# Modulation products of a fused two-block kernel taken from unsplit fp32 weights in four column groups, with six weight chunks in flight and two waits moved

## The reference

```python
for l in range(2):
    mod_lat = silu(c)     @ w_mod[l] + b_mod[l]    # [1024] @ [1024, 6144]
    mod_ctx = silu(c_ctx) @ w_mod[l] + b_mod[l]
    # shift, scale, gate for the mixer; shift, scale, gate for the MLP
    h = rms_norm(x, g) * (1 + scale) + shift
    x = x + gate * rms_norm(mixer(h), g_post)      # l=0: grid attention, l=1: gated linear attention
    x = x + gate * rms_norm(square(relu(h2 @ w_mlp_in)) @ w_mlp_out, g_post)
```

## Time and profile before

| | |
|---|---|
| executions | 2675.56, 2680.70, 2681.21 us (median 2680.7) |
| the profiled execution | 2680.21 us, of which the span of its instructions is 2678.6 |
| mean granted clock of PE | 0.933 of full speed |
| busy share of the span | PE 93%, PEld 83%, DVE 49%, ACT 39%, POOL 19% |
| DMA | 344.6 MB, 129 GB/s on average |

### The profile page before, as it was taken

The page is one execution under the profiler, slowest core; times in us unless marked ns, Lnnn a source line. Parts: engine busy times, 40 slices in busy tenths (PEclk is TensorE's granted clock), DMA queues, the critical chain, the costliest instruction groups (busy, mean ns, idle before and its releaser), DMA issues. The chain is left out here.

```text
span 2678.6 us, 38120 instructions
## 1 busy us (share of the span) xinstructions
PE 2484.1 (93%) x16773; PEld 2212.5 (83%) x16773; DVE 1323.7 (49%) x1609; ACT 1047.8 (39%) x1174; POOL 506.1 (19%) x464
## 2 busy tenths in 40 slices
PE   7998899999999997878999899998999979888998
PEld 7998889869999995456999877787888868657998
DVE  5655555566555555676655344343232244354443
ACT  3443343354434435555443334232322222443442
POOL 2113332302212211220221101012112211130211
PEclk9999999999999998799999899588999988978998
DMA  6554333344555555555555200021232222301552
GB/s 226 174 172 159 126 111 112 109 158 162 185 185 178 189 167 171 185 195 193 177 179 173 79 32 17 16 91 51 94 110 95 80 102 80 110 0 63 177 170 94
DMA packets 203055, 344.61 MB, mean 129 GB/s; under 512 B 8829, under 2 KB 65258, under 8 KB 202890
## 3 DMA queue, kind: packets, MB, share of 16 engines
q1 hardware_dynamic: 202890, 342.18, 37.9%
HBM read 341.11 MB, written 1.05 MB: 128 GB/s over the span
## 5 line engine op out<-in xcount | busy, mean ns | idle before, releaser
L435 DVE TENSOR_TENSOR WL<-raw,WH 128x2048 fp32r<-128x2048 f32 (+1 forms) x329 | 761.5, 2326 | 769.1 <-ACT WH L423 769.1
L423 ACT ACTIVATE WH<-raw 128x2048 fp32r<-128x2048 f32 (+1 forms) x329 | 610.2, 1865 | 406.3 <-PE PS L449 389.0
L449 PE MATMUL PS<-XH,WH 128*128 128x256 f32 (+1 forms) x2336 | 701.4, 300 | 24.7 <-DVE WL L435 14.9
L449 PE MATMUL PS<-XL,WH 128*128 128x256 f32 (+1 forms) x2336 | 695.5, 298 | 0.0
L449 PE MATMUL PS<-XH,WL 128*128 128x256 f32 (+1 forms) x2336 | 695.4, 298 | 0.0
L449 PEld LDWEIGHTS PS<-XH,WH 128*128 128x128 f32 x2336 | 454.2, 194 | 39.8 <-DVE WL L435 16.0
L449 PEld LDWEIGHTS PS<-XL,WH 128*128 128x128 f32 x2336 | 455.1, 195 | 10.2
L449 PEld LDWEIGHTS PS<-XH,WL 128*128 128x128 f32 x2336 | 454.6, 195 | 10.1
L449 PE MATMUL PS<-al,al 128*128 128x64 f32 (+7 forms) x1376 | 297.2, 365 | 17.2 <-DVE al L2821 9.3
L449 PE MATMUL PS<-WH,XH 128*128 128x256 f32 (+2 forms) x912 | 280.9, 308 | 11.8 <-DVE XL L606 7.9
L449 PE MATMUL PS<-WL,XH 128*128 128x256 f32 (+2 forms) x912 | 274.4, 301 | 0.0
(11 more groups left out here) (229 smaller groups left out, 2735.2 us busy)
## 6 DMA issues: line engine op xcount, KB each, us to landing
raw<-in_ffn_w_in SPq DMA_DIRECT2D x88, 1024.0 KB, 5.1
raw<-in_w_mod SPq DMA_DIRECT2D x48, 1024.0 KB, 5.1
raw<-in_ffn_w_out SPq DMA_DIRECT2D x40, 1024.0 KB, 5.0
raw<-in_a_w_in SPq DMA_DIRECT2D x36, 1024.0 KB, 4.9
raw<-in_w_mlp_in SPq DMA_DIRECT2D x32, 1024.0 KB, 5.4
raw<-in_w_mlp_out SPq DMA_DIRECT2D x32, 1024.0 KB, 5.0
raw<-in_gla_w_in SPq DMA_DIRECT2D x12, 1024.0 KB, 5.9
raw<-in_attn_w_qkv SPq DMA_DIRECT2D x6, 1024.0 KB, 6.1
```

What stands on the lines that cost most here:

```text
L423: act.e.activation(self.WH[j % NW][:, 0:nk * nn], self.raw[j % NRAW][:, 0:nk * nn], ACT.Copy).then_inc(*self.hi.up(j))
L435: dve.e.tensor_tensor(self.WL[j % NW][:, 0:nk * nn], self.raw[j % NRAW][:, 0:nk * nn], wh.bitcast(F32), ALU.subtract).then_inc(*self.lo.up(j))
L449: return self.pe.e.matmul(out, l, r, start=start, stop=stop, skip_group_check=skip)
```

## The change

- Six `raw` slots in place of three. The first three loads are unchanged; later ones wait until PE's matmuls on chunk c-6 are done (`lin`), where they waited for DVE's split of chunk c-3 (`lo`).
- `WL` of a chunk is written over its raw data (same address), and three separate `WL` buffers go.
- Chunks of the modulation are not split. A list `parted` numbers the others, and `WH` slots rotate by that number. `act_begin` and `dve_begin` skip modulation chunks.
- `CS` is plain fp32, 8 k-tiles of 32 columns, cleared by POOL; silu writes columns 0 and 1 directly. The copy and the subtraction for its split go.
- A modulation chunk is four fp32 matmuls, one for each k-tile j, from the raw chunk, each with 32 columns of `CS`, into partitions 32j to 32j+31 of the bank. Only the two chunks of a product are summed in PSUM; the four groups are summed in `turn`, which now takes all 128 partitions of `MR` and has `SEL` ones at rows 0, 32, 64, 96 and 1, 33, 65, 97. ACT's copy to `MR` has 128 partitions in place of 4.
- In the dilated stage a score with `tb` = 0 claims one bank.
- `grid_sp()` and `gla_sp()` stand ahead of chunk grid+5 and gla+5.
- `TRI` lies in a part of the constants that is free late in the program, and is loaded in `gla_sp()`.

```diff
-NRAW = 3
+NRAW = 6
 NW = 3
+FIRST = 3
...
-    c[0:4, SEL:SEL + 2] = np.array([[1, 0], [0, 1], [1, 0], [0, 1]], np.float32)
+    c[0:128:32, SEL] = 1.0
+    c[1:128:32, SEL + 1] = 1.0
...
-        self.WL = [f(f"WL{i}", 2048, F32R)[:] for i in range(NW)]
+        self.WL = [sb(f"WL{i}", [128, 2048], F32R, self.raw_at + 8192 * i)[:] for i in range(NRAW)]
...
+        self.TRI = sb("TRI", [128, 256], I32, self.cst_at + 2048)[:]
...
-        self.CS = f("CS", 32, F32R)[:].rearrange("p (k m) -> p k m", k=KT)
-        self.MR = sb("MR", [4, 512], F32, take(2048))[:]
+        self.CS = f("CS", 256)[:].rearrange("p (k m) -> p k m", k=KT)
+        self.MR = f("MR", 512)[:]
...
-        for c in range(NRAW, len(self.stream)):
-            if c == at + 2:
+        for c in range(FIRST, len(self.stream)):
+            if c == at + 5:
                 self.grid_sp()
-            if c == gla + 2:
+            if c == gla + 5:
                 self.gla_sp()
...
-            self.sp.wait_ge(self.lo, c - NRAW)
+            self.sp.wait_ge(self.lin, c - NRAW)
...
     def pe_chunk(self, src, nk, nn, tag=""):
+
         c = len(self.stream)
         self.stream.append((src, nk, nn, tag))
-        s = c % NW
         view = lambda t: t[:, 0:nk * nn].rearrange("p (k n) -> p k n", k=nk)
-        return c, view(self.WH[s]), view(self.WL[s])
+        if tag == "mod":
+            return c, view(self.raw[c % NRAW]), None
+        self.parted.append(c)
+        return c, view(self.WH[(len(self.parted) - 1) % NW]), view(self.WL[c % NRAW])
...
-            while self.act_split < min(self.act_begun + AHEAD - (held if i + 1 == n else 0), len(self.stream)):
-                j = self.act_split
+            while self.act_split < len(self.parted) and self.parted[self.act_split] < self.act_begun + AHEAD - (held if i + 1 == n else 0):
+                q = self.act_split
+                j = self.parted[q]
                 _, nk, nn, _ = self.stream[j]
                 act.wait_ge(self.raws[j % NRAW], j)
-                if j >= NW:
-                    act.wait_ge(self.lin, j - NW)
-                act.e.activation(self.WH[j % NW][:, 0:nk * nn], self.raw[j % NRAW][:, 0:nk * nn], ACT.Copy).then_inc(*self.hi.up(j))
+                if q >= NW:
+                    act.wait_ge(self.lin, self.parted[q - NW])
+                act.e.activation(self.WH[q % NW][:, 0:nk * nn], self.raw[j % NRAW][:, 0:nk * nn], ACT.Copy).then_inc(*self.hi.up(j))
...
+        pool.e.memset(self.CS, 0.0).then_inc(*self.ones.up("cond"))
...
-            act.e.activation(cs[:, :, i], self.COL[:, 221 + 8 * i:229 + 8 * i], ACT.Silu).then_inc(*self.a_step.up(("cond", i)))
-        act.wait_ge(self.a_step, ("cond", 1))
-        act.e.activation(self.CS[:, :, 0:2], cs, ACT.Copy).then_inc(*self.a_step.up("cond"))
+            act.e.activation(self.CS[:, :, i], self.COL[:, 221 + 8 * i:229 + 8 * i], ACT.Silu).then_inc(*self.a_step.up(("cond", i)))
...
-                m = self.mm(PS[:, b2, 2 * i:2 * i + 2], self.MR[0:4, i * 128:i * 128 + 128], self.CST[0:4, SEL:SEL + 2], True, True)
+                m = self.mm(PS[:, b2, 2 * i:2 * i + 2], self.MR[:, i * 128:i * 128 + 128], self.CST[:, SEL:SEL + 2], True, True)
...
-                    for k in range(4):
-                        cs, kt = self.CS[:, k0 + k, :], k0 + k
-                        both = lambda: self.mm(PS[0:4, b, :], cs, wh[:, k, :], kt == 0, kt == 7, True)
-                        upper = lambda: self.mm(PS[0:2, b, :], cs[:, 0:2], wl[:, k, :], False, False, True)
-                        for part in ((both, upper) if kt < 7 else (upper, both)):
-                            m = part()
+                    for j in range(4):
+                        m = self.mm(PS[32 * j:32 * j + 32, b, :], self.CS[:, k0 + j, :], wr[:, j, :], k0 == 0, k0 == 4, True)
...
-                    act.e.activation(self.MR, self.PS[0:4, b, :], ACT.Copy).then_inc(*self.evac.up(("mod", l, n)))
+                    act.e.activation(self.MR, self.PS[:, b, :], ACT.Copy).then_inc(*self.evac.up(("mod", l, n)))
...
-            self.pe_bank(b)
-            self.pe_bank(b + 1)
+            banks = [b, b + 1] if tb else [b]
+            for x in banks:
+                self.pe_bank(x)
...
-            self.empties([b, b + 1], (self.maxed, ("dil", hs, s)))
+            self.empties(banks, (self.maxed, ("dil", hs, s)))
...
-        sp.e.dma_start(self.CST[:, 0:512], A["const"][:, RESET:RESET + 512]).then_inc(*self.ld_masks.up("gla"))
+        sp.e.dma_start(self.CST[:, 0:512], A["const"][:, RESET:RESET + 512]).then_inc(*self.ld_masks.up("reset"))
+        sp.e.dma_start(self.TRI, A["tri"]).then_inc(*self.ld_masks.up("gla"))
```

More of the change, by code:

```diff
@@ L205, in place @@
         self.XL = [self.XLB[:, h] for h in range(2)]
+        self.raw_at = at
         self.raw = [f(f"raw{i}", 2048)[:] for i in range(NRAW)]
         self.WH = [f(f"WH{i}", 2048, F32R)[:] for i in range(NW)]
-        self.WL = [f(f"WL{i}", 2048, F32R)[:] for i in range(NW)]
+        self.WL = [sb(f"WL{i}", [128, 2048], F32R, self.raw_at + 8192 * i)[:] for i in range(NRAW)]
         h_at = take(49152)
@@ L217, in place @@
         self.rstd = f("rstd", 512)[:]
+        self.cst_at = at
         self.CST = f("CST", CONST_W)[:]
+        self.TRI = sb("TRI", [128, 256], I32, self.cst_at + 2048)[:]
         self.FRQ = f("FRQ", 48)[:]
-        self.TRI = f("TRI", 256, I32)[:]
         self.ONES = f("ONES", 128)[:]
@@ L318, in tensor_program @@
     def tensor_program(self):
-        self.plan, self.stream = self.stream, []
+        self.stream, self.parted = [], []
         self.bank, self.bank_of = [[] for _ in range(8)], {}
@@ L429, in dve_begin @@
             self.dve_begun += 1
-            while self.dve_split < min(self.dve_begun + AHEAD - (held if i + 1 == n else 0), len(self.stream)):
-                j = self.dve_split
+            while self.dve_split < len(self.parted) and self.parted[self.dve_split] < self.dve_begun + AHEAD - (held if i + 1 == n else 0):
+                q = self.dve_split
+                j = self.parted[q]
                 _, nk, nn, _ = self.stream[j]
                 dve.wait_ge(self.hi, j)
-                wh = self.WH[j % NW][:, 0:nk * nn]
-                dve.e.tensor_tensor(self.WL[j % NW][:, 0:nk * nn], self.raw[j % NRAW][:, 0:nk * nn], wh.bitcast(F32), ALU.subtract).then_inc(*self.lo.up(j))
+                wh = self.WH[q % NW][:, 0:nk * nn]
+                dve.e.tensor_tensor(self.WL[j % NRAW][:, 0:nk * nn], self.raw[j % NRAW][:, 0:nk * nn], wh.bitcast(F32), ALU.subtract).then_inc(*self.lo.up(j))
                 self.dve_split += 1
@@ L644, in start_sp @@
         self.ld_rows.name("rows")
-        for c in range(NRAW):
+        for c in range(FIRST):
             self.load_weights(c)
@@ L649, in start_sp @@
         sp.e.dma_start(self.FRQ, A["freq"]).then_inc(*self.ld_consts.up("freq"))
-        sp.e.dma_start(self.TRI, A["tri"]).then_inc(*self.ld_consts.up("tri"))
         self.ld_consts.name("consts")
@@ L724, in late_act @@
         act.e.activation(self.hs, self.ang_r, ACT.Sin, scale=0.5).then_inc(*self.a_step.up("half"))
-        cs = self.small[:, 72:88].rearrange("p (k s) -> p k s", s=2)
         act.wait_ge(self.col, "all")
+        act.wait_ge(self.ones, "cond")
         for i in range(2):
-            act.e.activation(cs[:, :, i], self.COL[:, 221 + 8 * i:229 + 8 * i], ACT.Silu).then_inc(*self.a_step.up(("cond", i)))
-        act.wait_ge(self.a_step, ("cond", 1))
-        act.e.activation(self.CS[:, :, 0:2], cs, ACT.Copy).then_inc(*self.a_step.up("cond"))
+            act.e.activation(self.CS[:, :, i], self.COL[:, 221 + 8 * i:229 + 8 * i], ACT.Silu).then_inc(*self.a_step.up(("cond", i)))
     def late_dve(self):
@@ L791, in late_dve @@
         t.then_inc(*up("tables"))
-        c2s = self.small[:, 72:88].rearrange("p (k s) -> p k s", s=2)
-        dve.wait_ge(self.a_step, "cond")
-        dve.e.tensor_tensor(self.CS[:, :, 2:4], c2s, self.CS[:, :, 0:2].bitcast(F32), ALU.subtract).then_inc(*up("cond"))
     def swiglu_pe(self, s):
@@ L2803, in chunks @@
             dec = self.gla_dec(h, d)
-            dve.wait_ge(self.ld_consts, "consts")
+            dve.wait_ge(self.ld_masks, "gla")
             dve.wait_ge(self.p_step, ("gla", "blank", 1))
```

6 lines of the change are left out of this document (3 added, 3 removed).

## The result

The changed kernel takes 2592.36 us (median of 4 runs, 2588.86 to 2594.11) beside 2679.9 us for the one before on the same chip: a ratio of 0.9674, with a 95% interval of 0.9658 to 0.9691. The prediction said 2592. The sum is right; several of its terms are not, and how they came to cancel is what the experiments are about.

A forecast was written before the change was run, and what follows sets the result against it. PE, busy for 93% of the span, was taken as the bound, with softmax-chain waits in the latent stage; savings 60.5 + 7 + 7 + 10 + 4 = 88.5 us off 2680.21 gave 2592 us, likeliest range 2560 to 2620 (0.70).

The forecast's parts named there:

- Bank 3: Dilated scores: an even score no longer claims bank 3, so transposes and scores wait less; 7 us saved (3 to 12).
- Dilated fills: Eight modulation chunks in 545 to 600 us, each cheaper on PE; 7 us saved (5 to 9).
- The latent stage: Six latent-attention stretches, 1033 to 1252 us: 60.5 us saved, 20.1 in the first two and 40.4 in the other four.
- the clock: Latent stretches: PE, asked for less, stands at 1.2 GHz longer; 2627 us; chance 0.13 shared with two at a time.
- The two other products: Products at 1783 and 2180 us: cheaper chunks and a split fewer ahead of DVE's spread; 4 us saved (2 to 6).
- gla_sp(): Near 2190 us: loads issued ahead of it let the spread PE waits for come earlier; 10 us saved (8 to 11).
- At nothing: Parts of the change priced at no time, among them six raw slots instead of three.
- 59 us for each us of a chunk: Slope over 48 modulation chunks: kernel time per us of chunk price at full clock, used to price rivals.
- two at a time: Modulation products: only two column groups overlap, 1.89 us a chunk; 2643 us; chance 0.13 shared with a lower clock.
- no overlap: Modulation products: column groups never overlap, 3.6 us a chunk; 2715 us, slower; chance of slower 0.05.
- The rival of program order: Modulation products: one group's high and low instructions can't overlap, 2.32 us a chunk; 2658 us; chance 0.04.
- Only the part on the softmax chain counts: Splits dropped for 48 chunks free 91 us of ACT and 112 of DVE; only the softmax-chain part saves time.

The follow-up runs named there:

- two groups: The changed kernel with k-tile j of a modulation chunk in column group j mod 2, so two sums in PSUM instead of four: 2599.35 us, ratio 0.9701.
- four slots: The changed kernel with four raw slots instead of six, WL still written over its raw chunk: 2612.10 us, ratio 0.9747.

## Why the prediction was right, and where it was not

The time came out within 1 us of the sum, and that closeness is luck: terms missed by 13.5 us one way and by 14 us the other.

- *Bank 3, "7 of 13.7 (3 to 12)"*: 18 us, shown twice. The mechanism was right; the term was mis-sized since it counted waits and expected some to come back. Nothing came back, and the half-clock stretch behind each wait came on top.
- *Dilated fills, 7*: 8.
- *The latent stage, 60.5*: 53.2, which is 55.4 in the two windows, of which 2.3 are gone again by 1275 us. The last four stretches took 115.1 us where I had 115.7. The first two took 48.4 instead of 42.7, with idle time about as left (10.0 beside 9) and the clock at 0.72: a chunk cost 1.45 us, not 1.27, and the other work 21.0, not 18.5. One of the prediction's own signs of being wrong, a clock below 0.75 in the latent stage, came true in these two. The rival "the clock" was no case apart; it is in both windows of this stage. In the four others idle time fell further than I had left it (16.3 for 20) and the lower clock took it back.
- *The two other products, 4*: no saving can be told there. No run undid the new place of grid_sp() or of `TRI`; the two traces show no lasting step at either place.
- *gla_sp(), 10*: 11.5 in the trace, 10.8 when it was undone, of which 7 us last to the end.
- *At nothing, six slots*: false. They are worth 40 us, since an unsplit chunk holds its slot for longer. The sum did not suffer, because I had forecast stretches as if no load were late, and with six slots none is.
- *"59 us for each us of a chunk"*: false below 1.9 us, where it was 8, and high above it: 78 us for 1.7, 46. It fixed the price of each rival, so "two at a time: 2643" would have been missed by 44 us had it come true, and "no overlap: 2715" by 38. That last one would have been level with the kernel before, not slower.
- *The rival of program order at L2614, "1.9 us"*: that is no overlap at all. Four instructions of the low half stand ahead of four of the high, so in program order one pair would overlap: 6x0.21+0.39 = 1.65 us. The row's 1.1 rules that out as well.
- *"Only the part on the softmax chain counts"* for the splits: they are worth 69 us where I had counted some 16 of idle time for them in the latent stage, and the cheap product, measured against two groups, 7. I had the credit the wrong way round. One size of error hid another: too little for bank 3 (11), too much for the latent stage (7) and the other products (5), too little for gla_sp() and the fills (1.5 and 1).

Undone one at a time the parts come to 69 + 40 + 18 + 7 = 134 us of 88, so some of what each is worth rests on the others. Bank 3 has no share in that, since it is worth 18 us in either kernel; gla_sp() and the slots have some, as four slots show. How much lies between the splits and the slots was not run.

## What to carry to other kernels

Price a wait on PE with the half-clock stretch behind it: look at the spacing of equal matmuls after it, not at the table of waits alone (here 13 us of waits were worth 18). Before making PE's work cheaper, see whether it stands between waits; there its time is partly what holds the clock up (0.65 to 0.94 in the dilated fills with splits), and taking work off the engines that make PE wait comes first. When an operation no longer frees a buffer early, ask for how long the buffer is now held, even where its reader does less.

## What the runs showed of the hardware that was not expected

- fp32 matmuls of 32 output columns in four column groups run wholly side by side: 1.07 us for four with 512 columns, 3.62 in one group, starts 7 ns apart.
- Column groups do not wait for each other in program order: with k-tiles 0 and 1 in the first group and 2 and 3 in the second a chunk takes 1.92 us, as when they alternate (1.91).
- A kernel can get faster by doing its matmuls in a slower way: 2660.99 to 2648.99 us with products of 1.9 instead of 1.07 us, as the granted clock of the latent stage rose from 0.69 to 0.91 and 0.87.
